# A decoder trunk on one core: products of the second and third norm started on the unnormalised residual

## The reference

```
...
    for i in range(DEPTH):
        j = i // N_MIXERS
        shift, scale, gate = ada_modulation(c, ada_w[i, 0], ada_b[i, 0])
        h = rms_norm(x) * (1.0 + scale) + shift
        if i % N_MIXERS == 0:
            y = forgetting_attention(h, fox_w_in[j], fox_b_f[j], fox_w_o[j])
        else:
            y = latent_attention(h, mla_w_a[j], mla_g_q[j], mla_g_kv[j],
                                 mla_w_uq[j], mla_w_ukv[j], mla_w_o[j])
        x = x + gate * y
        shift, scale, gate = ada_modulation(c, ada_w[i, 1], ada_b[i, 1])
        h = rms_norm(x) * (1.0 + scale) + shift
        x = x + gate * conv_gated_mlp(h, ffn_w_in[i], ffn_conv_w[i], ffn_conv_b[i], ffn_w_out[i])
    return rms_norm(x) * final_g
```

## Time and profile before

| | |
|---|---|
| median of 3 runs | 1329.35 us (1329.33 to 1330.15) |
| the profiled execution's own time | 1328.97 us |
| its span, first to last instruction | 1327.2 us |
| PE busy | 1276.1 us, 96% |
| weight loads (PEld) | 995.2 us, 75% |
| DVE busy | 829.6 us, 63% |
| ACT busy | 541.2 us, 41% |
| mean granted TensorE clock | 0.988 |

### The profile page before, as it was taken

The page is one execution under the profiler, slowest core; times in us unless marked ns, Lnnn a source line. Parts: engine busy times, 40 slices in busy tenths (PEclk is TensorE's granted clock), DMA queues, the critical chain, the costliest instruction groups (busy, mean ns, idle before and its releaser), DMA issues.

```text
span 1327.2 us, 18009 instructions
## 1 busy us (share of the span) xinstructions
PE 1276.1 (96%) x6239; PEld 995.2 (75%) x6239; DVE 829.6 (63%) x1262; ACT 541.2 (41%) x970; POOL 8.8 (1%) x23
## 2 busy tenths in 40 slices
PE   6999999998999999999999899999899999999997
PEld 3677777676888888788877666667688888888886
DVE  3656656766888878754446666664666666663232
ACT  5544444434333333322233566563434444432222
POOL 2000000000000000000000000000000000000000
PEclk7999999999999999999999999999999999999998
DMA  9523423342556656556332111123233333333331
GB/s 310 179 64 96 159 86 121 109 130 73 182 186 192 196 174 195 179 182 198 120 91 48 34 32 38 30 58 95 63 97 95 95 95 95 99 99 91 101 93 72
DMA packets 230601, 154.30 MB, mean 116 GB/s; under 512 B 27773, under 2 KB 221778, under 8 KB 227474
## 3 DMA queue, kind: packets, MB, share of 16 engines
q1 hardware_dynamic: 230546, 153.55, 38.6%
HBM read 151.43 MB, written 2.10 MB: 116 GB/s over the span
## 4 chain that ended last, share of the span: by engine, by line
PE 87%; DVE 6%; ACT 3%; issue 2%; SPq 2%; DMA 1%; ACTq 0%; DVEq 0%
PE pj L1433 75%; PE ov L1713 3%; PE tr L1685 2%; PE sc L1657 2%; PE sc L1669 1%; SPq L459 1%; DVE tmp L1059 1%; DVE hl L1046 1%; DVE nmax L1122 1%; ACT wh L606 1%; ACT tmp L730 1%; PE ov L1507 1%; DMA first_ada<-in_ada_w_dram 1%; DVE wl L968 1%; PE ov L1599 0%
## 5 line engine op out<-in xcount | busy, mean ns | idle before, releaser
L968 DVE TENSOR_TENSOR wl<-raw,wh 128x1024 fp32r<-128x1024 f32 (+2 forms) x214 | 234.3, 1095 | 306.2 <-ACT wh L606 305.7
L1433 PE MATMUL pj<-hh,wh 128*128 128x512 f32 x992 | 397.0, 400 | 14.9 <-DVE hl L1046 7.1
L606 ACT ACTIVATE wh<-raw 128x1024 fp32r<-128x1024 f32 (+2 forms) x214 | 204.5, 956 | 472.9 <-PE pj L1433 472.7
L1433 PE MATMUL pj<-hh,wl 128*128 128x512 f32 x992 | 387.2, 390 | 0.0
L1433 PE MATMUL pj<-hl,wh 128*128 128x512 f32 x992 | 386.9, 390 | 0.0
L1433 PEld LDWEIGHTS pj<-hh,wh 128*128 128x128 f32 x992 | 186.3, 188 | 62.5 <-DVE hl L1046 13.3
L1433 PEld LDWEIGHTS pj<-hh,wl 128*128 128x128 f32 x992 | 186.2, 188 | 39.5
L1433 PEld LDWEIGHTS pj<-hl,wh 128*128 128x128 f32 x992 | 186.6, 188 | 36.0 <-DVE hl L1046 1.1
L1433 PE MATMUL pj<-gh,wh 128*128 128x512 f32 x512 | 202.9, 396 | 0.7 <-DVE wl L968 0.7
L1433 PE MATMUL pj<-gh,wl 128*128 128x512 f32 x512 | 200.1, 391 | 0.0
L1433 PE MATMUL pj<-gl,wh 128*128 128x512 f32 x512 | 199.7, 390 | 0.0
(11 more groups left out here) (175 smaller groups left out, 1018.0 us busy)
## 6 DMA issues: line engine op xcount, KB each, us to landing
raw<-in_ffn_w_in_dram SPq DMA_DIRECT2D x88, 512.0 KB, 3.8
ada_w_sb<-in_ada_w_dram SPq DMA_DIRECT2D x40, 1024.0 KB, 5.1
raw<-in_ffn_w_out_dram SPq DMA_DIRECT2D x32, 448.0 KB, 3.6
raw<-in_fox_w_in_dram SPq DMA_DIRECT2D x24, 512.0 KB, 3.8
first_ada<-in_ada_w_dram SPq DMA_DIRECT2D x16, 512.0 KB, 9.0
raw<-in_ffn_w_out_dram SPq DMA_DIRECT2D x16, 512.0 KB, 3.8
raw<-in_fox_w_o_dram SPq DMA_DIRECT2D x8, 512.0 KB, 4.1
raw<-in_mla_w_o_dram SPq DMA_DIRECT2D x8, 512.0 KB, 3.8
```

The lines of the kernel that those rows point to most:

```text
L606: act.activation(wh[:, n0 % 2, 0:kt, :], raw[:, n0 % 2, 0:kt, :], ACT.Copy).then_inc(w_hi, 1)
L968: dve.tensor_tensor(wl[:, n0 % 2, 0:kt, :], raw[:, n0 % 2, 0:kt, :], f32(wh[:, n0 % 2, 0:kt, :]), ALU.subtract).then_inc(w_lo, 1)
L1433: ins = pe.matmul(bank_[:, :], (wl if term == 2 else wh)[:, s, kt, :], (rl if term == 1 else rh)(kt), start=start and j == 0, stop=stop an ...
```

## The change

**Two norms.** For norms 2 and 5, while the projection before is still running, each finished residual tile is multiplied by its `1 + scale` column and split into high and low part (`u`): one ACT instruction behind the square, one DVE instruction (`u_low`) behind the sum of squares, 8 of each a norm. PE (`norm_late` in place of `norm_over` and `two_tiles`) runs the first two output tiles on u, with the mean's and the spread's matmuls between them and without the idle products. ACT copies the two sums to SBUF (`z_take`), DVE multiplies them by the spread root (`scaled`), and ACT adds a column (`z_shift`): the shift's own product with the weights. DVE forms that product's partial sums from the raw weights, 8 dependent instructions of 128x128 for each of the two tiles (`shift_sum`), and two one-column matmuls finish it. From the third tile on, the stage uses h as before, which is still made for all eight tiles; the splits of the third and fourth weight chunk now stand inside `modulated` on DVE and ACT. The first pair of the second MLP is written out ahead of the loop.

**Second attention.** In b = 2 the weight split comes behind the copy of the transposes on ACT, and on DVE behind maximum, normalisation and the copy of k; in b = 3 it comes at the end of the DVE step.

The diff, cut:

```diff
@@ ACT
+            def z_take(j, C, T):
+                act.wait_ge(mm, C + j + 1)
+                act.activation(z_tile(j), PJ[(T + j) % 2][:, :], ACT.Copy).then_inc(z_t, 1)
+            def modulated_late(k, n, C, T):
+                act.wait_ge(mod_ok, k)
+                for kt in range(DT):
+                    high(k, kt)
+                    if kt == 2:
+                        z_take(0, C, T)
+                        split(C + 2)
+                z_take(1, C, T)
+                act.wait_ge(c_p, 1 if n == 2 else 2)
+                act.activation(shift_c[:, :], SC[1][:, 0:2], ACT.Copy).then_inc(c_s, 1)
+                split(C + 3)
+            def z_shift(j, n):
+                act.wait_ge(c_s, 1 if n == 2 else 2)
+                act.activation(z_tile(j), z_tile(j), ACT.Identity, bias=shift_c[:, j:j + 1]).then_inc(z_c, 1)
...
                 act.activation(sqb[j % 2], src, ACT.Square).then_inc(ev_a, 1)
+                if norm_n in U0:
...
+                    act.activation(u_tile(norm_n, m, True), src, ACT.Identity, scale=s1).then_inc(u_hi, 1)
...
+                    act.activation(early[:, 7:8], eps[:, 0:1], ACT.Silu)
+                    act.wait_ge(h_lo, DT * 4)
+                    for side in range(2):
+                        act.wait_ge(z_s, side + 1)
+                        z_shift(side, 5)
+                        act.activation(tmp[:, 2 * side, :], z_tile(side), ACT.Identity, bias=ccol(l, 3, side * FFT),
+                                       scale=ccol(l, 2, side * FFT)).then_inc(ev_a, 1)
...
+                if v is not None and v < 8:
+                    r = MLA_TR * (v // QB) + tr_at(v % QB)
+                    turned(v // QB % 2, v % QB, R + r, (R_MLA + r) % 2)
                 if fill and b == 2:
                     split_after(n0, t, 4, nxt)
@@ DVE
+                def scaled(j):
+                    dve.wait_ge(z_t, (0 if k == 2 else 2) + j + 1)
+                    dve.tensor_tensor(z_tile(j), z_tile(j), OV[1][:, :], ALU.mult
+                                      ).then_inc(ev_d if k == 2 else z_s, 1)
...
+                    if late is not None:
+                        if kt == 3:
+                            split(late + 2)
                 low(DT - 1)
+                if late is not None:
+                    scaled(0)
+                    scaled(1)
+                    split(late + 3)
...
+            def shift_sum(n0, side, norm_n):
+                k, c0 = U_MOD[norm_n], C_SUM[norm_n] + side * DT
+                dve.wait_ge(raw_in[n0 % 2], landed(n0, 0, 0))
+                for kt in range(DT):
+                    w, col, to = raw[:, n0 % 2, kt, :], mod[:, k, kt:kt + 1], shift_w[:, side, :]
+                    if kt:
+                        dve.wait_ge(c_acc, c0 + kt)
+                        ins = dve.scalar_tensor_tensor(out=to, in0=w, scalar=col, in1=to, op0=ALU.mult, op1=ALU.add)
+                    else:
+                        ins = dve.tensor_scalar(to, w, col, None, ALU.mult)
+                    ins.then_inc(c_acc, 1)
@@ PE
+            def norm_late(n, tile_n, C, T):
...
+                mean_most(n)
+                bank_free(T)
+                part(0, 0, 2)
+                mean_last(n, tile_n)
+                part(0, 2, 4)
+                spread(n)
+                pe.wait_ge(c_acc, C_SUM[n] + 2 * DT)
+                for side in range(2):
+                    ins = pe.matmul(SC[1][:, side:side + 1], shift_w[:, side, :], ones[:, 0:1], start=True, stop=True)
+                ins.then_inc(c_p, 1)
+                part(0, 4, DT)
+                bank_free(T + 1)
+                part(1, 0, DT)
...
-            norm_over(2, T_DOWN0 + DT - 1)
-            two_tiles(C_MA, T_MA, DT * 2)
+            norm_late(2, T_DOWN0 + DT - 1, C_MA, T_MA)
...
-            norm_over(5, T_MLAO + DT - 1)
+            norm_late(5, T_MLAO + DT - 1, C_UP1, T_UP1)
```

More of the change, by code:

```diff
@@ L202, in tile, with u_tile, h_tile, z_tile @@
             return g[:, t * S:(t + 1) * S] if isinstance(t, int) else g[:, bass.ds(t * S, S)]
+        def u_tile(n, m, high):
+            if n == 2:
+                g = hh if high else hl
+                return g[:, m, :] if isinstance(m, int) else g[:, bass.ds(m, 1), :]
+            return tile(gh if high else gl, m + DT)
+        def h_tile(k, kt, high):
+            if k == 2:
+                return tile(gh if high else gl, kt)
+            return (hh if high else hl)[:, kt, :]
+        shift_w = diag[:, 0:2 * P].rearrange("p (s q) -> p s q", q=P)
+        def z_tile(j):
+            return tmp[:, 4 + j, :]
         def pt_off(h, kb, b):
@@ L842, in mlp @@
                 else:
-                    with act.Fori(0, FFT // 2 - 1) as i:
+                    act.activation(early[:, 7:8], eps[:, 0:1], ACT.Silu)
[5 more added lines that the diff above has]
+                                       scale=ccol(l, 2, side * FFT)).then_inc(ev_a, 1)
+                    act.wait_ge(ev_d, T + 1)
+                    act.activation(tmp[:, 0, :], tmp[:, 0, :], ACT.Silu).then_inc(silu_s, 1)
+                    pair(0, 1, None)
+                    with act.Fori(1, FFT // 2 - 1) as i:
                         act.activation(early[:, 7:8], eps[:, 0:1], ACT.Silu)
@@ L1206, in step @@
                     square_add(i * 2 + j, j, i * 2 + (T + j), norm_n)
+                    if norm_n in U0:
+                        u_low(i * 2 + j, norm_n)
+                        if nxt is not None and j == 0:
+                            shift_sum(C + DT + 1, 1, norm_n)
                 dve.memset(ssq[:, :], 0.0).then_inc(ssq_s, 1)
+                if norm_n in U0:
+                    dve.wait_ge(mod_ok, U_MOD[norm_n])
                 if C == C_FOXO:
@@ L1223, in mlp, with pair @@
                 C, T = C_UP[l], T_UP[l]
-                def pair(i, par, nxt):
+                def pair(i, par, nxt, scaled=False):
                     m = i * 2 + par
@@ L1250, in mlp @@
                 if l:
-                    with dve.Fori(0, FFT // 2 - 1) as i:
+                    pair(0, 0, None, True)
+                    pair(0, 1, None)
+                    with dve.Fori(1, FFT // 2 - 1) as i:
                         for par in range(2):
@@ L1276, in down @@
                             split_after(C + j, i, 6, nxt)
+                        if j % 3 == 2 and norm_n in U0:
+                            u_low(i * 2 + j // 3, norm_n)
+                        if nxt is not None and j == 4 and norm_n in U0:
+                            shift_sum(C + 3 * DT + 1, 1, norm_n)
                         if l == 0:
@@ L1333, in _ @@
                 dve.wait_ge(ssq_s, s0 + j + 1 + (1 if j >= KVRT else 0))
-                dve.tensor_tensor(ssq[:, :], ssq[:, :], tmp[:, 5, :], ALU.add).then_inc(ssq_s, 1)
+                dve.tensor_tensor(ssq[:, :], ssq[:, :], tmp[:, 3, :], ALU.add).then_inc(ssq_s, 1)
                 if j == KVRT:
@@ L1345, in _ @@
             latents_lo(QRT, KVRT)
-            kt = tmp[:, 5, :]
+            kt = tmp[:, 3, :]
             bk = PJ[T_KR % 2]
@@ L1393, in mla_step @@
                     mla_take_k(t * 4 + (n0 + 1), 1 - j)
+                    split_after(n0, t, 4, nxt)
+                if fill and b == 3 and nxt is None:
+                    split_after(n0 + 1, t, 4, nxt)
                 if nxt is not None and s == 8:
@@ L1496, in norm_over, with u_h, u_l, part @@
                 idle_products(5)
+            def norm_late(n, tile_n, C, T):
+                def u_h(kt):
+                    return u_tile(n, kt, True)
+                def u_l(kt):
+                    return u_tile(n, kt, False)
+                def part(j, a, e):
+                    for kt in range(a, e):
+                        pe.wait_ge(u_lo, U0[n] + kt + 1)
+                        product(C + j, 0, 0, 3 * kt, 3 * kt + 3, u_h, u_l, PJ[(T + j) % 2])
+                mean_most(n)
[11 more added lines that the diff above has]
+                part(1, 0, DT)
             def idle_products(count):
@@ L1855, in _, with ma_h, ma_l @@
             mlp(0)
-            norm_over(2, T_DOWN0 + DT - 1)
-            two_tiles(C_MA, T_MA, DT * 2)
+            norm_late(2, T_DOWN0 + DT - 1, C_MA, T_MA)
+            def ma_h(kt):
+                return h_tile(2, kt, True)
+            def ma_l(kt):
+                return h_tile(2, kt, False)
             for j in range(2, QRT + KVRT + 1):
-                bank_free(T_MA + j)
+                if j < 4:
+                    pe.wait_ge(z_t, j - 1)
+                else:
+                    bank_free(T_MA + j)
                 half = 12 if C_MA + j == C_KR else 3 * DT
-                product(C_MA + j, 0, 0, 0, half, h_h, h_l, PJ[(T_MA + j) % 2])
+                for kt in range(half // 3):
+                    if j == 2:
+                        pe.wait_ge(h_lo, DT * 2 + kt + 1)
+                    product(C_MA + j, 0, 0, 3 * kt, 3 * kt + 3, ma_h, ma_l, PJ[(T_MA + j) % 2])
                 if j == KVRT:
```

103 lines of the change are left out of this document (72 added, 31 removed).

## The result

The changed kernel takes 1334.1 us at the median of 7 runs (1332.2 to 1334.6), against 1329.4 (1329.3 to 1330.9) for the kernel before on the same chip: ratio 1.0027, 95% interval 1.0017 to 1.0037. It is slower, by 0.27% by the ratio (3.6 us), while the medians alone lie 4.7 us apart. The prediction said 1325.4, faster, with a range of 1321.2 to 1329.9; the measured time lies 4.2 us above its upper end. The profiled run took 1332.21 us, with a span of 1330.4 against 1327.2.

What follows compares the result with a forecast made beforehand. The prediction took PE, with 87% of the chain that ended last, as the bound and its idle waits as the gain; 6.8 + 2.0 - 3.1 - 1.7 = 4.0 us gained gave 1325.4 us, range 1321.2 to 1329.9.

Steps and rivals of the forecast that it cites:

- Second norm, +2.0: Second norm: the fourth tile of the next stage starts at 711.9 instead of 713.87, 2.0 us gained.
- Second attention, +6.8: Second attention's reordered splits: 0.9 us gained in each of six loop rounds, 0.7 at two places before, 6.8 us together.
- Third norm, -3.1: Third norm: last add 5.0 us later, second MLP's fifth tile at 974.9 instead of 971.78, 3.1 us lost.
- The clock, -1.7: PE's new idle stretches of 4.2 and 4.1 us: one of two brings 3.4 us at half rate, 1.7 us lost.
- The rival that ended slower: Shift sums ahead of the residual add: slower from 4.9 us a sum, 0.61 a step; 1334 at 0.7; chance 0.07.
- The short sums of the first rival: Both norms' shift sums take 2.2 us each, with no clock loss: 8.5 us gained, 1320.9 us; chance 0.22.
- the signs that the prediction named for being wrong: Sums over 0.6 or under 0.3 a step, a round less than 0.4 shorter, or second MLP's fifth tile earlier.
- the attention's wait moves only: Second attention: another wait replaces the removed one, half or more of 6.8 us lost, about 1328.5 to 1332; chance 0.15.

Runs made afterwards that it cites:

- e14: Changed kernel with idle products in all its new gaps (17 ahead of the latent mean, 14 ahead of the fifth tile, 8 and 3 in the third norm): 1328.04 us.
- e6: Changed kernel with seven of the eight multiply-and-adds of each shift sum left out, so the result is not the shift: 1327.40 us.
- e2: Kernel before with the attention's reorder alone, but on DVE the k/v split ahead of the v copy and `pair_take`: 1326.45 us.
- e1: Kernel before with the attention's reordered splits alone, both norms as before: 1328.43 us.
- e11: Changed kernel with sums on GpSimd, silu table early, q split ahead of the k copy, k/v split between v copy and `pair_take`: 1324.18 us.
- e5: Kernel before with the third norm's change alone, attention and second norm as before: 1335.22 us.
- e9: Changed kernel with ACT's silu table loaded earlier, in an idle gap behind the third norm's fourth modulated tile: 1331.20 us.
- e12: Changed kernel with PE's mean of the first latents moved from ahead of the fourth latent tile to behind it: 1329.23 us.

## Why the prediction was wrong

The failed steps are two: the k/v split's later place in the attention was taken to cost nothing, and the half clock was priced at 1.7 us where it cost 4.6 in the profiled run. e14, with full clock at all these places, lets the structure be read apart from the clock. Against before, its attention starts at 738.78 instead of 740.66, leaves at 890.64 instead of 893.99, and its fifth tile starts at 970.41 instead of 971.78.

- *Second norm, +2.0.* Right: 740.66 - 738.78 = 1.9 gained. The sums (2.9 for 3.2), the late root, the idle of 4.2 ahead of the mean: each came as worked out, within 0.3. But of the 1.7 us that the normalisation is late the sums' share is 0.45 by e6, where 0.8 was worked out.
- *Second attention, +6.8.* Wrong, and the larger part of the error: 893.99 - 890.64 - 1.9 = 1.5 gained. The step that failed is the sentence that the k/v split moves later too "but its product stands two blocks of queries away". That was taken for room enough. The product does open in the next head's second block, but PE works ahead of DVE and was ready for it at 790.40 - 0.53 = 789.87, while the split had moved not by one instruction but behind a copy and `pair_take`, which waits for ACT (789.23). With that split put ahead of both, still behind maximum and normalisation, e2 gains 3.7 us where e1 gains 1.7. A smaller miss: counted from the b = 2 scores, the q product came 3.39 us on before (796.62 - 793.23) and 2.60 now (796.04 - 793.44), 0.8 gained for 0.9. It is the k/v product's wait of 0.53 that takes most of this back. Even e2 and e11, with that wait gone, gain 0.68 and 0.76 a round: in e11 PE's own work, busy for 18.27 of 18.57 us, is what binds.
- *Third norm, -3.1.* Right in its mechanism, too large: 971.78 - 970.41 = 1.4 is left of the 3.4 gained until then, so 2.0 are lost. Counted from the projection's last product, the last add was 4.3 late, not 5.0, as each sum was 0.3 shorter.
- *The clock, -1.7.* The mechanism was named, the size was wrong: I took one stretch of 3.4 us of two possible. In the profile there is a double one at the second norm, worth 2.9 (the fourth tile's stage ends 1.0 later than before where e14's ends 1.9 earlier), and a single one behind the fifth tile, 1.7: 4.6 in all. The rule of the Trainium skill that I weighed (TensorE: Matmul & The Clock Gate, the section on what's actually happening) has every idle stretch of some microseconds bring the clock down. It was nearer to this than my choice: both stretches, of 4.15 and 3.71 us, were followed by the half clock. What it leaves out here is that shorter ones of 1.55 to 2.7 us were too, in some runs.

The four differences are 5.3, 0.1, -1.1 and 2.9 us, together 7.2: from 4.0 us gained to 3.2 lost, as the two profiled spans have it. A median run has 1.9 us more than the profiled one; that a further slow stretch at the third norm's waits is the reason is suggested by e5, e9 and e12, whose profiles show it, and not shown for the changed kernel itself. The rival that ended slower, with a chance of 0.07, had the right sign for the wrong reason: a step took 0.39 (a sum's steps start at 683.76, 684.15, 684.54), not over 0.61. The short sums of the first rival, at 0.29 a step, did not come either: an instruction alone took 0.352. Of the signs that the prediction named for being wrong one came, a round less than 0.4 shorter.

Of the rivals "the attention's wait moves only", with 0.15, had the attention right: over half of the 6.8 is lost to waits for the splits that now stand last, and e1, with the reorder alone, comes to 1328.4 where it said 1328.5 to 1332. The changed kernel's 1334.1 lies beyond it, by the clock. I gave it too little because I counted the 0.87 us of room at one place of DVE and did not follow the second split that the same edit moves.

## What to carry to other kernels

Where an edit moves a helper's call in an order that several steps share, follow every call that it moves, with what it is moved past and who waits for it next; here the second, smaller split undid the first one's gain. And where PE gets through its work earlier, but what it waits for next comes no earlier, count the stretch in which it then stands idle and price the half clock behind it: in the profiled run it cost 4.6 us, more than the 2.0 that the third norm lost by its late start. A few products that compute nothing, or a better order (the mean behind the tile that is ready), win it back.
